# Norms over heads inside the projections, rotation tables on GpSimd, result copies on VectorE

## What is computed

```
def rms_norm_2(x, gain):
    y = xf * lax.rsqrt(jnp.mean(xf * xf, axis=-1, keepdims=True) + NORM_EPS)
    return (y * gain.astype(F32)).astype(x.dtype)

def memory_cross_attention(h, mem_n, w_q, w_kv, q_gain, k_gain, w_o):      # 4 heads of 256, twice
    q = rms_norm_2((h @ w_q).reshape(b, t, MEM_HEADS, MEM_HEAD_DIM), q_gain)
    k, v = jnp.split(mem_n @ w_kv, 2, axis=-1)        # mem_n = rms_norm_2(mem, norm_mem)
    k = rms_norm_2(k.reshape(b, m, MEM_HEADS, MEM_HEAD_DIM), k_gain)
    p = jax.nn.softmax(jnp.einsum('bthd,bmhd->bhtm', q, k) * MEM_HEAD_DIM ** -0.5, axis=-1)
    return jnp.einsum('bhtm,bmhd->bthd', p, v).reshape(b, t, D_MODEL) @ w_o

def diff_attention(...):                              # 8 heads of two times 64, once
    q, k, v = jnp.split(h @ w_qkv, 3, axis=-1)
    q = rms_norm_2(q.reshape(b, t, DIFF_HEADS, 2, DIFF_HEAD_DIM), q_gain)
    k = rms_norm_2(k.reshape(b, t, DIFF_HEADS, 2, DIFF_HEAD_DIM), k_gain)
```

## Time and profile before

| | |
|---|---|
| median of three executions | 2943.56 us (2926.44, 2945.67, 2943.56) |
| profiled execution, own time | 2930.94 us |
| its span, first to last instruction | 2929.1 us |
| mean granted TensorE clock | 0.937 of 2.4 GHz |
| TensorE / VectorE / ScalarE / GpSimd busy | 2601.7 / 1915.5 / 1515.6 / 90.4 us |
| HBM read | 561.2 MB, 194 GB/s over the span |

### The profile page before, as it was taken

One profiled execution on the slowest core, in us unless ns is written; L12 is line 12 of the kernel. 1 busy time (PEld: TensorE's weight loads), 2 busy tenths in 40 slices (PEclk: granted clock), 3 DMA queues, 4 the chain that ended last, 5 costly groups with the idle time before them and its releaser, 6 DMA issues. The chain is left out here.

```text
span 2929.1 us, 37611 instructions
## 1 busy us (share of the span) xinstructions
PE 2601.7 (89%) x13581; PEld 2117.6 (72%) x13582; DVE 1915.5 (65%) x2368; ACT 1515.6 (52%) x1875; POOL 90.4 (3%) x115
## 2 busy tenths in 40 slices
PE   6889887997869698998978879998998999999998
PEld 5678765776765486887757657777887777777777
DVE  4555545796668544555455459885454889888888
ACT  3544335443221343444444347774443777777776
POOL 0000011000143000000100000000000000000000
PEclk9999988998887898999989879999998999999999
DMA  8346512455200541464414239995554899999996
GB/s 276 133 153 191 164 58 94 144 179 164 68 2 1 201 158 58 159 198 147 144 40 147 72 115 365 327 361 188 183 182 152 313 319 348 330 357 330 358 328 225
DMA packets 333583, 566.24 MB, mean 193 GB/s; under 512 B 21929, under 2 KB 126712, under 8 KB 333080
## 3 DMA queue, kind: packets, MB, share of 16 engines
q1 hardware_dynamic: 333464, 564.59, 56.9%
HBM read 561.19 MB, written 6.50 MB: 194 GB/s over the span
## 5 line engine op out<-in xcount | busy, mean ns | idle before, releaser
L1240 DVE TENSOR_TENSOR weights_split<-ring,weights_split 128x1024 fp32r<-128x1024 f32 x676 | 819.3, 1224 | 266.5 <-ACT weights_split L1235 229.2
L1315 PE MATMUL ps<-weights_split,expert_split 128*128 128x512 f32 x3864 | 914.6, 394 | 25.9 <-DVE expert_split L1411 17.7
L1235 ACT ACTIVATE weights_split<-ring 128x1024 fp32r<-128x1024 f32 x676 | 715.3, 1061 | 353.1 <-PE ps L1315 341.8
L1315 PEld LDWEIGHTS ps<-weights_split,expert_split 128*128 128x128 f32 x3864 | 722.3, 189 | 193.2 <-DVE weights_split L1240 38.2
L289 DVE TENSOR_TENSOR weights_split<-ring,weights_split 128x2048 fp32r<-128x2048 f32 x182 | 413.4, 2272 | 418.0 <-ACT weights_split L280 417.4
L280 ACT ACTIVATE weights_split<-ring 128x2048 fp32r<-128x2048 f32 x182 | 345.0, 1896 | 436.4 <-PE ps L460 259.0
L459 PE MATMUL ps<-normed_split,weights_split 128*128 128x512 f32 x1248 | 446.4, 400 | 25.5 <-PEq L342 25.1
L460 PE MATMUL ps<-normed_split,weights_split 128*128 128x256 f32 x1248 | 353.7, 283 | 0.0
L459 PEld LDWEIGHTS ps<-normed_split,weights_split 128*128 128x128 f32 x1248 | 239.6, 192 | 82.1 <-issue 27.5
L365 PE MATMUL ps<-weights_split,hidden_split 128*128 128x512 f32 x1032 | 244.4, 393 | 17.4 <-DVE weights_split L289 9.3
L460 PEld LDWEIGHTS ps<-normed_split,weights_split 128*128 128x128 f32 x1248 | 239.9, 192 | 1.4
(11 more groups left out here) (393 smaller groups left out, 2339.0 us busy)
## 6 DMA issues: line engine op xcount, KB each, us to landing
ring<-moe_w_gate SPq DMA_DIRECT2D x112, 1024.0 KB, 5.2
ring<-moe_w_up SPq DMA_DIRECT2D x112, 1024.0 KB, 5.3
ring<-moe_w_down SPq DMA_DIRECT2D x112, 1024.0 KB, 5.2
ring<-mlp_w_up SPq DMA_DIRECT2D x32, 1024.0 KB, 5.5
ring<-mlp_w_down SPq DMA_DIRECT2D x32, 1024.0 KB, 5.0
ring<-xa_w_kv SPq DMA_DIRECT2D x16, 1024.0 KB, 5.2
ring<-moba_w_qkv SPq DMA_DIRECT2D x12, 1024.0 KB, 12.2
ring<-da_w_qkv SPq DMA_DIRECT2D x12, 1024.0 KB, 5.2
```

Source lines behind the costliest of these rows:

```text
L1235: nc.scalar.activation(split_piece(p, 0), ring_piece(p), ACT.Copy).then_inc(high.sem, 1)
L1240: nc.vector.tensor_tensor(split_piece(p, 1), ring_piece(p), split_piece(p, 0).bitcast(F32), ALU.subtract)\
L1315: last = nc.tensor.matmul(ps[:, banks[half][tt], :], stationary(s, k, tt), split_piece(p, i)[:, kk * NW:(kk + 1) * NW], start=(opens and n ...
```

## The change

1. New function `qkv_normed` in place of `qkv_products` and `grouped_norm`, in both cross attentions (`per_unit` 1, norm over 256) and in the differential attention (`per_unit` 4, norm over 64). Squares, sums (`pick`), inverse (`invert`), spreading (`spread_unit`) and products (`apply`) lie between the units of the projection. For `per_unit` 1, VectorE first adds the squares of the two blocks of a unit (`halves_added`), and the memory's norm is also done inside, after unit 0; its own stage is gone. The inverse is multiplied as two rounded halves in one matmul.
2. The doubling of the S5 tables moves from VectorE's rounds to GpSimd (`tables_pool`), which starts when the first turn is made. Angles, first turn and coefficients stay on VectorE.
3. In `attention` with heads of 64 the result copy moves from ScalarE to the end of VectorE's round.
4. Opening: the first layer's gain comes by a load of its own, ahead of the weight tiles; x is turned once it is there; the other parameters are turned and the bias row is made after x; ring slots 2 to 5 are issued here and not in the next stage; only one weight tile is split ahead of the norm's products (VectorE leaves the second to the next stage).
5. The latent attention's projection stage splits the first two tiles of the output projection at its end (`hi`, `lo` with taken + 3 + WS_BUFS).
6. In the differential attention GpSimd's scaling of the ALiBi table (eight instructions, L2962) and the lambda sums move from the norm's stage into the projection's.

```
+            core.hi(e, core.taken + (1 if opening else WS_BUFS))
...
+        for s in range(steps + 3 if pair else steps + 1):
...
+            if s >= 3 and pair:
+                t = s - 3
+                e.wait_ge(*outs.at(t + 1))
+                nc.vector.tensor_copy(oT[:, t, :], core.ps[:, 6 + t % 2, 0:T]).then_inc(*kept.up())
...
+def qkv_normed(core, per_unit, gain, qk, vN, memory=None, lead=None, pool=None):
+    one = per_unit == 1
+    size = 256 if one else 64
+    R = 32 if one else 64
...
+    SUMS, SPREAD = 6, (7, 7, 7, 7, 7, 2, 3, 6)
...
+    def pe(e):
+        def pick(u):
+            cols = slice(u // 4 * T, u // 4 * T + T)
+            if u == 0 and memory:
+                e.wait_ge(*mem_split.at(4))
+            if u == 4:
+                e.wait_ge(*roots.at(1))
+            if one:
+                e.wait_ge(*halves_added.at(u + 1))
+                first = u % 4 + 1
+                last = nc.tensor.matmul(ps[0:R, SUMS, cols], c("pick_all")[:, PICK - first:PICK - first + R],
+                                        both[:, u % 2, :], start=(u % 4 == 0), stop=(u % 4 == 3))
+            else:
+                e.wait_ge(*squares.at(u + 1))
+                first = 2 * (u % 4)
+                for t in range(2):
+                    last = nc.tensor.matmul(ps[32 * t:32 * t + 32, SUMS, cols],
+                                            c("pick")[:, PICK - first:PICK - first + 32],
+                                            sq[:, u % 2, t * T:(t + 1) * T], start=(u % 4 == 0), stop=(u % 4 == 3))
+            last.then_inc(*sums.up())
+        def spread_unit(j):
+            if j == 0:
+                e.wait_ge(*spreader_made.at(1))
+            if j % 4 == 0:
+                e.wait_ge(*inverse_.at(j // 4 + 1))
+            if 1 <= j <= 4:
+                e.wait_ge(*normed.at(j))
+            if j == 5:
+                e.wait_ge(*freed.at(8))
+            if j == 7:
+                e.wait_ge(*roots.at(2))
+            for t in range(2):
+                m = j % 4 if one else 2 * (j % 4) + t
+                last = nc.tensor.matmul(ps[:, SPREAD[j], t * T:(t + 1) * T], spreader[0:2 * R, m * P:(m + 1) * P],
+                                        split[0:2 * R, :], start=True, stop=True)
+            last.then_inc(*spread.up())
...
+        for u in range(8):
+            w = core.weights(e, t0 + u)
+            xs = core.XS if u < 4 else MS
+            if u >= 2:
+                e.wait_ge(*freed.at(u - 1))
+            if u == 4 and memory:
+                e.wait_ge(*mem_split.at(4))
+            for t in range(2):
+                for k in range(KD):
+                    last = wide_product(core, ps[:, 2 * (u % 2) + t, :], w, (ALL, k, slice(t * P, (t + 1) * P)),
+                                        xs, k, k == 0, k == KD - 1)
+            core.fill(last, bank=True, tile=True)
+            if u == 0 and memory:
+                for tt in range(TT):
+                    e.wait_ge(*mem_scaled.at(tt + 1))
+                    for k in range(KD):
+                        last = nc.tensor.transpose(ps[:, 4 + k // 2, k % 2 * T + tt * P:k % 2 * T + (tt + 1) * P],
+                                                   mem[:, tt, k * P:(k + 1) * P], c("ident"))
+                        if tt == TT - 1 and k % 2 == 1:
+                            last.then_inc(*mem_turned.up())
+            if u >= 1:
+                pick(u - 1)
+            if u >= 5:
+                spread_unit(u - 5)
+        for i in range(4):
+            half, j = i // 2, i % 2
+            if i == 2:
+                e.wait_ge(*freed.at(8))
+            w = core.weights(e, t0 + 8 + i)
+            for tt in range(TT):
+                for k in range(4):
+                    last = product(core, ps[:, v_bank(half, tt), :], w, (ALL, k, ALL), halves(MS),
+                                   (ALL, 4 * j + k, slice(tt * P, (tt + 1) * P)), j + k == 0, 4 * j + k == 7, tokens=True)
+                if j == 1 or tt == TT - 1:
+                    core.fill(last, bank=(j == 1), tile=(tt == TT - 1))
+            if i == 0:
+                pick(7)
+                spread_unit(3)
+            if i == 1:
+                spread_unit(4)
+            if i == 2:
+                for j in (5, 6, 7):
+                    spread_unit(j)
...
+        for i in range(12):
+            core.hi(e, min(t0 + i + 1 + WS_BUFS, t0 + 13))
+            if i < 8:
+                core.wait_bank(e, i)
+                if i >= 2:
+                    e.wait_ge(*freed.at(i - 1))
+                nc.scalar.activation(two(low[:, i % 2, :]), ps[:, 2 * (i % 2):2 * (i % 2) + 2, T:2 * T], ACT.Copy)\
+                    .then_inc(*low_kept.up())
+                e.wait_ge(*freed.at(i + 1))
+                if i >= 2:
+                    e.wait_ge(*(halves_added if one else sums).at(i - 1))
+                nc.scalar.activation(sq[:, i % 2, :], flat(qk[:, 2 * i:2 * i + 2, :]), ACT.Square).then_inc(*squares.up())
+            if i == 0 and memory:
+                for b in range(4):
+                    e.wait_ge(*mem_turned.at(b + 1))
+                    for j in range(2):
+                        k = 2 * b + j
+                        last = nc.scalar.activation(MS[:, 0, k, :], ps[:, 4 + b, j * T:(j + 1) * T], ACT.Identity,
+                                                    scale=mem_gain(k))
+                    last.then_inc(*mem_high.up())
+            if i == 4:
+                e.wait_ge(*sums.at(4))
+                nc.scalar.activation(root, ps[0:R, SUMS, 0:T], ACT.Sqrt, bias=eps(E_EPS256 if one else E_EPS64, R))\
+                    .then_inc(*roots.up())
...
+        def invert(phase):
+            e.wait_ge(*roots.at(phase + 1))
+            core.link(e, "dve", V.reciprocal(inv, root))
+            if phase:
+                e.wait_ge(*spread.at(4))
+            core.link(e, "dve", V.tensor_copy(split[0:R, :], inv))
+            V.tensor_tensor(split[R:2 * R, :], inv, split[0:R, :].bitcast(F32), ALU.subtract)\
+                .then_inc(*inverse_.up())
+        def apply(j):
+            e.wait_ge(*spread.at(j + 1))
+            if one:
+                for t in range(2):
+                    last = V.scalar_tensor_tensor(qk[:, 2 * j + t, :], qk[:, 2 * j + t, :], gain(2 * j + t),
+                                                  ps[:, SPREAD[j], t * T:(t + 1) * T], ALU.mult, ALU.mult)
+            else:
+                last = V.scalar_tensor_tensor(flat(qk[:, 2 * j:2 * j + 2, :]), flat(qk[:, 2 * j:2 * j + 2, :]),
+                                              gain(2 * j), ps[:, SPREAD[j], :], ALU.mult, ALU.mult)
+            last.then_inc(*normed.up())
...
+        for i in range(12):
+            core.lo(e, min(t0 + i + 1 + WS_BUFS, t0 + 13))
+            if one and 1 <= i <= 8:
+                u = i - 1
+                e.wait_ge(*squares.at(u + 1))
+                if u >= 2:
+                    e.wait_ge(*sums.at(u - 1))
+                V.tensor_tensor(both[:, u % 2, :], sq[:, u % 2, 0:T], sq[:, u % 2, T:2 * T], ALU.add)\
+                    .then_inc(*halves_added.up())
+            if i < 8:
+                e.wait_ge(*low_kept.at(i + 1))
+                V.tensor_tensor(qk[:, 2 * i:2 * i + 2, :], ps[:, 2 * (i % 2):2 * (i % 2) + 2, 0:T], two(low[:, i % 2, :]),
+                                ALU.add).then_inc(*freed.up())
+            if i == 0 and memory:
+                for b in range(4):
+                    e.wait_ge(*mem_high.at(b + 1))
+                    for j in range(2):
+                        k = 2 * b + j
+                        last = V.scalar_tensor_tensor(MS[:, 1, k, :], ps[:, 4 + b, j * T:(j + 1) * T], mem_gain(k),
+                                                      MS[:, 0, k, :].bitcast(F32), ALU.mult, ALU.subtract)
+                    last.then_inc(*mem_split.up())
+            if i in (4, 8):
+                invert(i // 4 - 1)
+            if 5 <= i <= 9:
+                apply(i - 5)
+            if i == 10:
+                for j in (5, 6, 7):
+                    apply(j)
+    stage(core, pe=pe, act=act, dve=dve, pool=pool, uses=12)
...
+    def tables_pool(self, e):
+        g, link = self.core.nc.gpsimd, self.core.link
+        t1, t2 = self.qt
+        link(e, "pool", g.memset(self.COS[:, :, 0:1], 1.0))
+        link(e, "pool", g.memset(self.SIN[:, :, 0:1], 0.0))
+        e.wait_ge(*self.turn_made.at(1))
+        tt = lambda out, x0, x1, op: link(e, "pool", g.tensor_tensor(out, x0, x1, op))
+        q = (self.co, self.si)
+        for level in self.LEVELS:
             count = min(ST, 512 // level)
-            for group in range(ST // count):
-                for part in range(2):
-                    if n == first:
-                        self.double(e, level, group * count, count, (part,))
-                    first += 1
+            for first in range(0, ST, count):
+                which = slice(first, first + count)
```

(47 more changed lines are left out.)

170 lines of the change are left out of this document (97 added, 73 removed).

## The result

The changed kernel takes 2979.56 us (median of four, 2977.34 to 2980.91) against 2942.56 for the kernel before. The ratio over all fast runs, which is not just the quotient of the two medians (1.0126), is 1.0137, interval 1.0105 to 1.0168: slower, by more than the 1% that can be told from no change. The forecast was 2969 us. The profiled execution took 2977.34 us against 2930.94, that is 46.4 us more, where the sum had +25.3.

A forecast was written before the change was run, and what follows sets the result against it. TensorE, busy 89% of the span, was the bound, through its waits and lower clock. +51.6 - 12.8 - 9.5 - 5.5 + 1.0 + 0.5 = +25.3 us gave 2956.2 profiled, 2968.9 with the median's 12.6 added; range 2938 to 2996.

The forecast's parts named there:

- The waits of the sums: Cross attentions: TensorE waits 4.7 us for VectorE's addition at each of eight sums, 37.8 us in one cross attention.
- Clock behind a wait: Cross attentions: each wait of a sum also lowers TensorE's clock, costing 1.7 us, 13.6 for eight waits.
- rival of twice the loss: Cross attentions: the clock falls for longer, twice the loss at each of 16 waits, +27 us, 2996; chance 0.12.
- the one of a clock that holds: Cross attentions: TensorE keeps its clock despite the waits, 27 us are not lost, 2942 us; chance 0.10.
- The sums themselves: One cross attention: eight sums of squares on TensorE add 3.6 us.
- Second cross attention: Forecast the same as the first cross attention: +25.8 us, with +51.6 for both.
- Differential attention: Norm moved into the products, without the addition: -12.8 us, between -17 and -9.
- Tables: S5 table doubling moved to GpSimd in the second MLP: -9.5 us, from -13 to +4.
- the rival in which it ends the MLP: Second MLP: GpSimd's table work ends last; at 155 us the stage is 14 us later, forecast 2982; chance 0.15.
- Opening: Start of the kernel: gain loaded apart, SP's bias store held behind ring tiles: -5.5 us, between -7.2 and -3.5.
- Result copy, latent stage: Copy on VectorE in the attentions: +1.0 us (-0.5 to +3). Tiles split ahead in the latent stage: +0.5 (-1 to +2.5).
- The rival in which the sums don't wait: Cross attentions: the addition is ready when a unit ends, 103 us less, 2866 us; chance 0.08.

The follow-up runs named there:

- sums_first: The changed kernel with VectorE's addition of the squares put ahead of the low half in its round: 2877.71 us, ratio 0.9796 to the kernel before.
- filled: The changed kernel with 20 needless products on TensorE ahead of five of the eight waits in each cross attention: 2949.86 us, ratio 1.0041.
- relaxed: On top of sums_first, TensorE takes the sums of units 0 and 4 and the first spreading one unit later: 2858.79 us, ratio 0.9740.
- copy_scalar: On top of sums_first, the result copy of the 64-wide heads is back on ScalarE: 2878.14 us, ratio 0.9800.
- diff_before: On top of sums_first, the differential attention has its products and its norm over heads apart, as before the change: 2889.87 us, ratio 0.9852.

## Why the prediction was right, and where its sizes were off

The direction was named with a chance of 0.43, the likeliest single outcome was put at "within 1%" (0.47), and 2979.6 lies inside 2938 to 2996. The mechanism stood as written; the sum fell 21 us short of the profiled difference (46.4 for 25.3) and 12 short of that of the medians (37.0). That the absolute forecast, 2969, is only 11 us off owes something to luck: it rests on the 12.6 us between the profiled execution before and its median.

- *The waits of the sums.* Right to the instruction: `hi`, `lo`, addition, at all eight sums, 4.72 us (5.8 at the first of each stretch, 4.81 once in each) for 4.7. sums_first shows the cause, since only the order changed.
- *Clock behind a wait.* Right in kind and in size: the six units and two tiles of v behind the eight waits took 59.5 us from start to end, and at full clock, with 5.71 for two units, 5.81 for four and 5.73 for a tile, it is 46.1. That makes 1.7 us for each wait, as forecast. filled shows it by itself (some 1.7 for the unit). The rival of twice the loss and the one of a clock that holds are both out.
- *The sums themselves: the term that was most off.* I took eight sums at 0.45, 3.6 us, from a stage with a matmul list of its own. From start to next start they took 7.9, because each one stands directly behind the wait and so in the half-clock stretch: 1.06 us for the pair in L1097, against 0.62 in relaxed. Spreading took 4.2 for 2.4 (0.72 us a unit at half clock, 0.43 at full). The turnings took 1.7 for 3.6. All units and tiles together took 83.8 us for 68.4 before, 15.4 more; the 2 us of it that are not the 13.4 of clock are mostly ends of units, which the next unit's start used to overlap by 0.16 us. With the stage that shrank from 26.58 us to a change of stages of 0.98 (-25.6, which is not the -25.6 of the prediction: that has other terms in it) the first stretch has -25.6 + 39.0 + 15.4 + 7.9 + 4.2 + 1.7 = +42.6, as in the trace; the forecast had +35.7.
- *Attention behind it.* A gain that I had not listed: 18.66 us for 20.66, since it now begins at full clock (and 18.65 for 20.44 in the second).
- *Second cross attention.* I used the first one's norm stage (26.58 us) for both. The second had 23.76 before, so there was 2.8 us less to win; hence +34.4.
- *Differential attention.* -11.5 for -12.8. The wait for root and split was there, in two pieces, 1.1 and 2.0 us for 2.4; in the second half TensorE waited 1.1 us (I had 0.8), there for a product of VectorE's (L1230). The unit behind the first two took 8.2 us from start to end, some 2.5 of them clock, for which I had no term; the sums, 0.56 us a unit, took 4.5 for 7.1 and made up for it.
- *Tables.* -7.0 for -9.5. GpSimd worked 126 us from the first turn on (554.0 to 679.6, busy for 117.5; forecast 115 to 155) and ended at 170.5 (160 to 200), so the rival in which it ends the MLP was not met. `lo` spread from 2.29 to 3.38 us (forecast 2.3 to 3.5), and TensorE still waited 6.0 us for it, of forecast 5.1.
- *Opening.* -4.2 for -5.5: SP last, as said, but 1.3 us later, with one more tile to issue behind the store.
- *Result copy, latent stage.* No difference that can be told (copy_scalar) for +1.0, and 0.0 for +0.5. The latent stage's parts were right one by one (+5.8 for +5.7, -3.8 for -4.9), and the output projection gave 2.0 us of clock where I had 0.3.
- *The rival in which the sums don't wait* was priced at 2866 us; sums_first, which makes it true by one exchange, has 2878.

My bounds for one cross attention, +12 to +40, held both (+30.7 and +34.4), but I took the middle of them. Behind a wait every instruction should have been costed at the slow rate, the small ones too: with the sums and the spreading as measured (4.3 and 1.8 us more in each stretch) the sum comes out at +37.5, over 1%.

## What to carry to other kernels

When work is threaded into another loop, ask of each inserted instruction what stands in front of it on its own engine, and whether that can only run after the unit which it holds up. Here 0.42 us of ready work behind a blocked one cost 102 us in all, and exchanging the two turned a loss of 1.4% into a gain of 2.0%. If TensorE must wait anyway, count what follows, and every small matmul just behind the wait, at the lower level of the clock; here needless products in the pause gave 2.0 us back for each pause.

## What the runs showed of the hardware

The granted clock also moves where nothing was changed, by several microseconds. The projections into the latent space take 21.12 us before and 24.55 after, with the same instructions and TensorE busy throughout. The windows of the changed kernel, the whole stretch and its two parts:

```profile
359.50:384.05 24.55, 24.55 (x168) 24.46 (x168) 0.76 (x1) 2.52 (x5) 0.00 (x0) 0.78 0.26 86
```

```profile
365.00:378.70 13.70, 13.70 (x120) 13.70 (x119) 0.76 (x1) 2.52 (x5) 0.00 (x0) 1.00 0.24 78
378.80:384.05 5.25, 5.25 (x26) 5.16 (x25) 0.00 (x0) 0.00 (x0) 0.00 (x0) 0.50 0.00 0
```

The clock falls from 1.00 (2.4 GHz) to 0.50 (1.2 GHz) during the 48 products of 128 x 8 columns, in which TensorE never paused. In the trace of before the same products ran at 1.00 (window 363.5 to 380.5). Over the twelve traces this stretch is 21.1 to 21.7 us in six and 24.5 to 24.7 in the other six. The Trainium skill, TensorE: Matmul & The Clock Gate, Part 1, names the half-rate state "Idle/cold". Here the measurement says more: the busy share of this row is full and the clock still 0.50, so a full busy share in a profile does not promise full clock.

The RWKV and S5 stretch is untouched too. Its windows in sums_first and in diff_before, each up to the norm of the first cross attention:

```profile
714.66:1013.11 298.45, 235.48 (x2353) 190.59 (x2353) 187.56 (x276) 73.26 (x106) 62.27 (x71) 0.80 0.20 62
```

```profile
714.71:998.35 283.64, 217.89 (x2353) 177.41 (x2353) 187.31 (x276) 73.27 (x106) 61.29 (x71) 0.86 0.20 65
```

With the same 2353 matmuls it takes 298.5 us at a clock of 0.80 and 283.6 at 0.86. The other ten traces lie between, at 286.8 to 293.3 us. What sets which of them an execution gets was not settled. Such differences are as large as the 5 to 10 us by which medians here differ more than the edited stages do; that they make them up is not shown, since each kernel has one trace. It is why the stages are compared here and not the totals alone.
